# Recurrence of a two-block kernel: VectorE's 32x32 block transposes make the transposed triangular inverse up to level 16

## What is computed

```python
def _wkv_scan(S0, decay, k, v, kk, a, r, reverse):
    def step(S, inp):
        w_t, k_t, v_t, kk_t, a_t = inp[:5]
        sa = jnp.einsum('bhvk,bhk->bhv', S, -kk_t)
        S = (S * w_t[:, :, None, :] + sa[..., None] * (kk_t * a_t)[:, :, None, :]
             + v_t[..., None] * k_t[:, :, None, :])
        y = jnp.einsum('bhvk,bhk->bhv', S, inp[5]) if len(inp) == 6 else None
        return S, y
    S, ys = lax.scan(step, S0, xs, reverse=reverse)
```

## Time and profile before

| | |
|---|---|
| median of 3 runs | 4052.66 us (4052.08 to 4056.37) |
| the profiled execution's own time | 4049.61 us |
| its span, first to last instruction | 4047.8 us |
| busy in the span | PE 3586.4 us, DVE 1590.9, ACT 1017.6, POOL 1061.3 |
| the 16 units | from about 2709 to 3557 us of the span |

### The profile page before, as it was taken

How to read it: one execution, slowest core, us unless ns; L and a number is a source line. 1 busy time by engine, 2 the same in 40 slices (tenths; PEclk the granted TensorE clock), 3 DMA queues, 4 the chain that set the end, 5 groups by cost and what they waited for, 6 DMA issues and landing times.

```text
span 4047.8 us, 84008 instructions
## 1 busy us (share of the span) xinstructions
PE 3586.4 (89%) x37130; PEld 2666.9 (66%) x37130; DVE 1590.9 (39%) x2806; ACT 1017.6 (25%) x1590; POOL 1061.3 (26%) x696
## 2 busy tenths in 40 slices
PE   8996798778868899989999989859999999989997
PEld 3454476623326677768888845438888888867885
DVE  3255542411127755433333420314555455523333
ACT  2032232211114244331111031322322332223221
POOL 0002341121122100032222120025555454424441
PEclk9997899889979899989999989979999999989998
DMA  4207153179961100111111123420000000011221
GB/s 172 94 32 294 44 207 127 74 277 369 362 249 37 42 1 1 69 79 63 63 63 63 63 76 132 157 73 3 14 14 14 14 14 14 4 63 73 100 98 42
DMA packets 64600, 379.35 MB, mean 94 GB/s; under 512 B 12906, under 2 KB 12906, under 8 KB 26352
## 3 DMA queue, kind: packets, MB, share of 16 engines
q1 hardware_dynamic: 40032, 291.52, 18.7%
q0 software_dynamic: 20608, 68.82, 4.4%
q10 hardware_dynamic: 3600, 13.63, 0.9%
HBM read 380.21 MB, written 44.04 MB: 105 GB/s over the span
## 4 chain that ended last, share of the span: by engine, by line
PE 75%; DVE 6%; POOL 6%; DMA 6%; ACT 3%; issue 2%; SPq 0%; DVEq 0%; ACTq 0%; POOLq 0%
PE psum L462 20%; PE psum L474 11%; PE psum L475 10%; PE psum L476 10%; PE psum L750 4%; DMA arena<-in_wall 3%; PE psum L2096 2%; PE psum L2827 2%; PE psum L2814 2%; PE psum L769 2%; PE psum L2123 2%; DMA ring<-in_wall 2%; PE psum L648 1%; PE psum L3116 1%; PE psum L2797 1%
## 5 line engine op out<-in xcount | busy, mean ns | idle before, releaser
L462 PE MATMUL psum<-arena 64*64 64x64 f32 (+4 forms) x14024 | 636.6, 235 | 57.1 <-POOL arena L3050 23.5
L462 PEld LDWEIGHTS psum<-arena 64*64 64x64 f32 (+2 forms) x14024 | 511.3, 139 | 151.2 <-issue 109.9
L492 POOL TENSOR_TENSOR ring_low<-ring,slab_high 128x2048 fp32r<-128x2048 f32 x66 | 303.9, 4617 | 648.7 <-ACT slab_high L485 648.6
L474 PE MATMUL psum<-h_high,slab_high 128*128 128x512 f32 (+1 forms) x1056 | 378.1, 358 | 16.6 <-DVE h_low L512 10.0
L475 PE MATMUL psum<-h_low,slab_high 128*128 128x512 f32 (+1 forms) x1056 | 376.9, 357 | 0.0
L476 PE MATMUL psum<-h_high,ring_low 128*128 128x512 f32 (+1 forms) x1056 | 376.5, 356 | 0.0
L462 PE MATMUL psum<-arena,ring 128*128 128x512 f32 (+3 forms) x992 | 368.4, 531 | 2.1 <-DVEq L1269 1.3
L462 PEld LDWEIGHTS psum<-arena,ring 128*128 128x128 f32 (+2 forms) x992 | 184.2, 187 | 184.0 <-issue 173.5
L474 PEld LDWEIGHTS psum<-h_high,slab_high 128*128 128x128 f32 x1056 | 201.4, 191 | 51.8 <-issue 10.6
L941 DVE TENSOR_TENSOR arena<-arena,psum 128x512 f32<-128x512 f32 x66 | 39.5, 599 | 486.1 <-PE psum L476 481.9
L476 PEld LDWEIGHTS psum<-h_high,ring_low 128*128 128x128 f32 x1056 | 201.5, 191 | 28.4
(11 more groups left out here) (433 smaller groups left out, 6241.1 us busy)
## 6 DMA issues: line engine op xcount, KB each, us to landing
ring<-in_wall SPq DMA_DIRECT2D x181, 1024.0 KB, 5.1
arena<-in_wall SPq DMA_DIRECT2D x96, 1024.0 KB, 12.1
moe_rows<-arena POOLq DMA_DIRECT2D x2, 6144.0 KB, 67.7
arena<-moe_rows ACTq DMA_DIRECT2D x24, 512.0 KB, 7.7
moe_out<-arena POOLq DMA_DIRECT2D x24, 512.0 KB, 9.1
arena<-spill POOLq DMA_DIRECT2D x8, 1024.0 KB, 5.3
spill<-arena POOLq DMA_DIRECT2D x2, 3072.0 KB, 17.7
filters<-arena POOLq DMA_DIRECT2D x2, 2048.0 KB, 6.6
```

The costliest lines, as they stand in the source:

```text
L462: last = L.eng.matmul(out, a, b, start=(i == 0), stop=(i == len(pairs) - 1))
L474: L.eng.matmul(out, a_hi, b_hi, start=(i == 0), stop=False)
L492: L.eng.tensor_tensor(m.low[:, n % SLOTS, :], m.ring[:, n % SLOTS, :], m.high_of(n).bitcast(F32), ALU.subtract).then_inc(m.sem("slab_split ...
```

## The change

It removes the score family `al,be`, POOL's two subtractions that began `B.ti`, and the product `transposed_tensor` at levels 2 to 16. In their place DVE transposes in blocks of 32x32: once per head from `B.tt` to `B.ti` to begin with (semaphores `inverse_begun`, `inverse_turned`), and at levels 2, 4, 8 and 16 from `B.ti` to `B.tt` behind the update of `B.ti`. Up to level 16 the inverse consists of diagonal blocks of 32 at most, so that block transposes give it whole. A block transpose handles 128 partitions x 384 columns, one head. At levels 4 to 32 the PE product waits for the transpose of its head; DVE waits for its own update before each transpose. At level 32 the product `transposed_tensor` is still made. With two score steps fewer, chain steps 8 to 11 now stand behind the four turns of `al` and `be` (`FIRST` = 8). The cut diff:

```diff
 def inverse_start_pool(L, m, B, u):
-        e.tensor_tensor(t, over(B.eye, TT), t, ALU.subtract).then_inc(m.sem("inverse"), 1)
-    for hh in range(2):
-        t = of_head(B.ti, hh)
-        L.eng.wait_ge(m.sem("starts_read"), L.nth("starts_read"))
-        e.tensor_tensor(t, over(B.eye, TT), t, ALU.subtract).then_inc(m.sem("inverse"), 1)
+        e.tensor_tensor(t, over(B.eye, TT), t, ALU.subtract).then_inc(m.sem("inverse_begun"), 1)
...
+def heads_columns(a, hh):
+    return a[:, TT * CH * hh:TT * CH * (hh + 1)]
+
+
+def inverse_turn_vector(L, m, dst, src, hh):
+
+    L.eng.transpose(heads_columns(dst, hh), heads_columns(src, hh)).then_inc(m.sem("inverse_turned"), 1)
+    return L.nth("inverse_turned")
...
-FIRST = 10
+FIRST = 8
...
 def unit_tensor(L, m, B, u, before, done, after, w2, g2):
-    for lhs, rhs, n in ((u.be, u.al, TT), (u.al, u.be, TT), (u.ka, u.al, TT), (u.be, u.rh, TX), (u.ka, u.rh, TX)):
+    for lhs, rhs, n in ((u.be, u.al, TT), (u.ka, u.al, TT), (u.be, u.rh, TX), (u.ka, u.rh, TX)):
...
-        for tiles in TURNS:
+        for half, tiles in enumerate(TURNS):
             turned.append(turn_pair_tensor(L, m, src, tiles))
-        if before is not None and k < 2:
-            chain_tensor(L, m, B, before, FIRST + k)
+            if before is not None and k < 2:
+                chain_tensor(L, m, B, before, FIRST + 2 * k + half)
...
             if lv == LEVELS[0]:
-                L.eng.wait_ge(m.sem("inverse"), L.nth("inverse", 1 if hh else 3))
-            for updated in inverse[hh]:
-                L.eng.wait_ge(*updated)
+                L.eng.wait_ge(m.sem("inverse_turned"), L.nth("inverse_turned"))
+            else:
+                L.eng.wait_ge(*inverse[hh])
             corner.append(squares_tensor(L, hh, lambda *at: [(square(B.nt, *at), square(B.ti, *at))]))
...
             L.eng.wait_ge(*corner[hh])
-            inverse[hh] = []
-            if lv != LEVELS[-1]:
-                inverse[hh].append(inverse_tensor(L, B, hh))
-            inverse[hh].append(transposed_tensor(L, B, hh))
+            if lv != LEVELS[0]:
+                L.eng.wait_ge(m.sem("inverse_turned"), L.nth("inverse_turned"))
+            inverse[hh] = inverse_tensor(L, B, hh) if lv != LEVELS[-1] else transposed_tensor(L, B, hh)
...
 def unit_vector(L, m, B, u, before, done, after):
...
-    for hh in range(2):
-        ti_read = read(of_head(B.ti, hh), masked(4 + d))
-        chain(2 + hh)
-        L.eng.wait_ge(*ti_read)
-        L.eng.sem_inc(m.sem("starts_read"), 1)
...
+            if k < 2:
+                chain(FIRST + 2 * k + half)
+    turned_back = []
+    for hh in range(2):
+        L.eng.wait_ge(m.sem("inverse_begun"), L.nth("inverse_begun"))
+        turned_back.append(inverse_turn_vector(L, m, B.ti, B.tt, hh))
     if done is not None:
         readout_centre_vector(L, m, B, done)
...
         for hh in range(2):
-            for dst, side in (((B.ti, d), (B.tt, 1 - d)) if lv != LEVELS[-1] else ((B.tt, 1 - d),)):
-                ps = L.next_bank()
-                L.eng.wait_ge(L.bank_full, L.fill)
-                o = side_of(dst[:, TT * CH * hh:TT * CH * (hh + 1)], lv, side)
-                e.tensor_tensor(o, o, side_of(ps[:, 0:TT * CH], lv, side), ALU.subtract).then_inc(L.bank_free, 1)
+            dst, side = (B.ti, d) if lv != LEVELS[-1] else (B.tt, 1 - d)
+            ps = L.next_bank()
+            if lv in (LEVELS[0], LEVELS[-1]):
+                L.eng.wait_ge(m.sem("inverse_turned"), turned_back[hh])
+            L.eng.wait_ge(L.bank_full, L.fill)
+            o = side_of(heads_columns(dst, hh), lv, side)
+            e.tensor_tensor(o, o, side_of(ps[:, 0:TT * CH], lv, side), ALU.subtract).then_inc(L.bank_free, 1)
+            if lv != LEVELS[-1]:
+                L.eng.wait_ge(*L.read_out)
+                turned_back[hh] = inverse_turn_vector(L, m, B.tt, B.ti, hh)
```

More of the change, by code:

```diff
@@ L3160, in unit_tensor @@
             at_bank += 1
-    akt = scores[4:6]
+    akt = scores[2:4]
     turned = []
@@ L3181, in unit_tensor @@
         removal_sum_tensor(L, m, B, after)
-    inverse = [[], []]
+    inverse = [None, None]
     for lv in LEVELS:
@@ L3209, in unit_tensor @@
     for hh in range(2):
-        L.eng.wait_ge(*inverse[hh][-1])
+        L.eng.wait_ge(*inverse[hh])
         solved.append(squares_tensor(L, hh, lambda *at: [(square(B.tt, *at), tok(B.altok, *at))]))
@@ L3217, in unit_tensor @@
         feats_tensor(L, p, lambda *at: [(tok(B.betok, *at), square(B.uv, *at)), (tok(B.katok, *at), tok(B.vtok, *at))])
-    for masked in scores[6:]:
+    for masked in scores[4:]:
         L.eng.wait_ge(*masked)
@@ L3235, in unit_scalar @@
             copy(dst[:, lo * P:hi * P], ps[:, :(hi - lo) * P], 1.0)
-        if before is not None and (dst is B.altok or dst is B.betok):
-            L.next_bank()
+            if before is not None and (dst is B.altok or dst is B.betok):
+                L.next_bank()
     if after is not None and after.d == 0:
@@ L3258, in unit_scalar @@
             L.next_bank()
-        for _ in range(4 if lv != LEVELS[-1] else 2):
+        for _ in range(2):
             L.next_bank()
@@ L3308, in unit_vector @@
     for hh in range(2):
-        ti_read = read(of_head(B.ti, hh), masked(4 + d))
+        read(of_head(B.akt, hh), masked(first))
         chain(2 + hh)
-        L.eng.wait_ge(*ti_read)
-        L.eng.sem_inc(m.sem("starts_read"), 1)
-    for hh in range(2):
-        read(of_head(B.akt, hh), masked(first))
-        chain(4 + hh)
     for k, dst in enumerate((B.rbt, B.rkt)):
@@ L3318, in unit_vector @@
             read(of_head(dst, hh, TX), masked(upto))
-            chain(6 + 2 * k + hh)
+            chain(4 + 2 * k + hh)
     if u.d == 0:
@@ L3323, in unit_vector @@
     for k in range(3):
[L3324 to L3327, removed]
+        for half in range(2):
+            L.next_bank()
+            if k < 2:
[4 more added lines that the diff above has]
+        turned_back.append(inverse_turn_vector(L, m, B.ti, B.tt, hh))
     if done is not None:
```

## The result

The changed kernel takes **4020.03 us** (median of 4 runs, 4014.85 to 4025.49), the kernel before in the same comparison 4052.37: a ratio of 0.9919, 95% interval 0.9902 to 0.9936. That is 32 us faster, inside the range of 3980 to 4034, and 21 us short of the 3999 forecast. The profiled execution took 4025.49 us, and TensorE's mean granted clock over the whole span fell from 0.937 to 0.917.

A forecast was written before the change was run, and what follows sets the result against it. PE was taken to bound units with d = 1, POOL's preparation behind the scan those with d = 0. 4049.6 minus 63 of work plus 10 for the clock gave 3996.6, with 3 for the median 3999 us; range 3980 to 4034.

The forecast's parts named there:

- What bounds the kernel: With d = 0 POOL's preparation: only gains before the scan count; with d = 1 all count, under 5.5 us behind it.
- Scores: Two TT score steps go, two chain steps move among the turns: net gain 1.0 us a unit, 1.4 in unit 0.
- Levels 2 and 4: Product families go ahead of the scan: level 2 gains 1.4 us, level 4 0.58 with d = 1, 0.39 with d = 0.
- Levels 8 and 16: Behind the scan, DVE sets the pace: a level takes 3.35 us instead of 4.38, a gain of 1.03, twice.
- T: Time of one DVE 128x384 block transpose, in no measured row: taken as 0.56 us, between 0.35 and 0.88.
- The sum: Gains over all units, without the clock: 5.0 us with d = 1, 2.8 with d = 0, together 63 us.
- The clock: Behind level 4, PE's waits lower the clock: one fall in three of 14 gaps, 2 us each, 10 us lost.
- rival 1: The clock falls at nearly every gap, also at a growing second wait: price 43 us, 4033; chance 0.14.
- Rival 2: DVE's transposes wait for POOL, 0.9 us each at levels 8 and 16: 26 us less gain, 4027; chance 0.10.
- Rival 3: An fp32 transpose streams several cycles per column, making the kernel slower: 4105 us at T = 1.75; chance 0.06.
- rival 4: The gain before the scan is eaten by another wait, leaving less than 0.2% (8 us); chance 0.03.

The follow-up runs named there:

- fill_all: Changed kernel plus idle matmuls in three TensorE waits (4 before d = 1 units, 3 before level 8, 3 before ACT's solutions with d = 0): 3981.76 us.
- scores_only: Kernel before with only the score family al,be and POOL's start of B.ti replaced by DVE's first transposes, chain steps moved; both products kept at all levels: 4035.52 us.
- levels_only: Kernel before with only the product family of levels 2 to 16 replaced by DVE's transposes; score family and POOL's start kept: 4032.94 us.
- ka_after: Changed kernel with POOL's first two instructions for the keys moved ahead of its wait for the decay scan: 3992.04 us.
- late_before: Kernel before with one extra, unused POOL instruction (1.47 us) ahead of the last operand instruction of seven d = 1 units: 4084.25 us.
- turn_twice: fill_all with every transpose of levels 8 and 16 done twice, one behind the other: 4018.39 us.

## Why the prediction was right, and where it was off

**What bounds the kernel, and where a gain counts: right.** With d = 0 the end of the unit stays 23.6 us behind the scan in before, after and fill_all alike, and what levels 8 and 16 gained there became the wait of 1.91 us for POOL. With d = 1 they gained 2.2, against 2.06. One reading was off without harm: the 3024.28 of the earlier trace rows is the first chain step, which stands behind the first score family. The scores of unit 6 start at about 3023.2, so POOL had 4.4 us to spare there and 3.4 to 4.4 in all units with d = 1, not 5.5. In after 1.3 to 2.8 are left, so the gain behind the scan still counted in full.

**Scores (1.0): right**, 1.02 with d = 0 in scores_only. **Levels 2 and 4 (1.8 with d = 0): right**, 1.9 in levels_only. **Levels 8 and 16 (3.35 us): 3.28**: the mask of the next level starts at 2944.23, 0.08 before the last transpose ends, so an overlap that I gave to the updates holds there too. **T (0.56): 0.574** as a mean in the changed kernel, and 0.61 from one transpose to the next. The estimate of 0.58 from the Trainium skill (VectorE: DVE Perf Modes, The three transpose paths) is nearer still, though the page measures bf16: these are fp32. Scores, level 2 and level 4 together were forecast at 2.8 with d = 0, and 2.86 were measured.

**The sum (63): right once the clock holds.** The profiled execution of fill_all is 4049.61 - 3982.40 = 67.2 us shorter than that of before. A pair of units takes 107.3 us before and 98.9 in fill_all, 8.4 less, against 7.8.

**The clock (10): the step that failed.** The prediction put the price in one place, "one fall in three of 14 such gaps", behind level 4. There it was even too dear: six falls of 3.5 to 4 us, of which three lie in units with d = 0 and are hidden behind POOL, and the other three cost 1.45, 1.1 and 1.1 (scan to next start 23.14, 22.78 and 22.80 against 21.69). The dear place is the one it called only a lost gain: PE's wait for POOL at the end of a unit with d = 0, and the wait for ACT ahead of it. Against fill_all, counted from POOL's end to the scan, after loses 4.3 to 4.8 us in units 1, 3, 5 and 7 and as much in unit 15 as a whole, 6.2 and 7.6 in units 9 and 11, into which the two long falls reach, and 1.2 in unit 13, where fill_all has its own fall of 3.4. That is 37.5; with the 3.7 behind level 4 it makes 41. The two profiled executions are 4025.49 - 3982.40 = 43.1 us apart, and 2.4 of these lie ahead of unit 0, where the kernels are the same. So the clock took back about 41 us where 10 were put down, and the work gained 67 where 63 were. The medians of the two kernels are 38 us apart.

That the time fell inside the range is in part luck: 4020 is nearer to rival 1's 4033 than to the 3999 forecast, and only the room given to a dear transpose (up to 4024) and to rivals 1 and 2 (up to 4034) made the range reach so far. The transpose cost what was forecast; the clock used up that room.

The fault in the reasoning can be named. I read from the earlier trace rows that a stretch with long waits is followed by half the clock, and used the 6.5 us of that row as its length. I did not ask, of the other wait that the change makes, what stands behind it. Behind it stand 9 us of 64x64 scores and chain steps (2962.91 to 2972.19 in unit 5) with hardly a gap, and the clock came back neither in them nor in the first turns, but at about 2978.5.

**Rival 1** was priced at 43 us for a fall at nearly every gap, and about 41 is what the clock cost, but from another sum: 6 of its 14 gaps behind level 4 brought a fall, and at all eight starts with d = 1 the clock was low. It named the second wait ("with d = 0 ACT copies the solutions only after the exponentials that wait for POOL") and gave it 2.5 us. The Trainium skill's passage (TensorE: Matmul & The Clock Gate, A second HAM failure mode: psum-queue depth-cycling), short idles between groups of matmuls that make the clock go up and down, fits: PE was busy for 1.59 of 3.5 us ahead of the fall in unit 5. The page's example is in bf16 with 512 columns, and it puts no figure on the loss.

**Rival 2** (transposes held by POOL) did not happen: at most 580 ns, beside POOL as well. But the mechanism exists at another instruction: the scan with its two inputs in SBUF is held, as ka_after shows. **Rival 3** (several cycles per column) did not happen, and neither did **rival 4**.

**What stays open.** Why the clock fell in units 5, 7 and 9 of scores_only, with a wait for POOL of at most 0.41 us, and not in the others or in before, no run tells. Nor does the length of the wait tell it behind level 4: PE waits 1.79 us ahead of level 8 in each of units 0 to 14 of after, and in six of them the clock fell. In the kernel before only two lengths were tried at the starts, 0.19 to 0.41 us (before) and 1.8 to 2.0 (late_before); where between them it tips isn't known.

## What to carry to other kernels

When an edit takes matmuls away, make two sums: the work that goes, and the waits of TensorE that grow, each with what stands behind it; a wait ahead of a long stage of small matmuls can cost more than it lasts (here waits of 1.3 to 1.9 us each brought some 14 us at half the clock, which cost about 4.4 us). Check the granted clock of the stage behind each wait in the profile after, not only over the span. Where TensorE has to wait anyway, idle matmuls that fit into the wait can hold the clock: here they turned a gain of 32 us into one of 68. Where the wait is gone they cost their own length (turn_twice).

## What the runs showed of the hardware

- Behind the fall at the start of unit 5 the clock stays low for 14 us although PE is busy for 13.82 of them with 64x64 matmuls and a few turns; other falls in the recurrence of after last from 3.5 to 28 us.
- PE shows it as a longer busy time, not as idle: 13.82 of 14 us busy at 0.51. The share of busy time reads such a stage as full.
- A DVE block transpose of 128x384 fp32 takes 574 ns on the mean (533 to 580) and isn't stretched by POOL beside it; a scan of 128x768 with two SBUF inputs is, from 1.72 to 2.65 us (unit 4 of ka_after).
- A matmul of 128x256 in fp32 takes 0.5 us (1.99 for four), so a few of them fill a wait of 2 us.
